# Spreading the inverse softmax sums of two attentions: one rounded, split operand for both heads instead of two fp32 matmuls

## What is computed

```python
def attend(q, k, v, bias=None, mask=None, sink=None):
    s = jnp.einsum('...qngd,...knd->...ngqk', q, k).astype(jnp.float32) * (HEAD_DIM ** -0.5)
    if bias is not None:
        s = s + bias.astype(jnp.float32)
    if mask is not None:
        s = jnp.where(mask, s, NEG_INF)
    if sink is not None:
        s = jnp.concatenate([s, sink_col], axis=-1)
    p = jax.nn.softmax(s, axis=-1)
    ...
    return jnp.einsum('...ngqk,...knd->...qngd', p.astype(v.dtype), v)
```

## Time and profile before

| what | us |
|---|---|
| median of three runs (lowest, highest) | 3851.95 (3849.77, 3854.59) |
| the profiled execution, its own time | 3849.42 |
| its span | 3847.3 |
| TensorE busy in the span | 3714.5 (97%) |
| VectorE busy | 2176.0 (57%) |
| ScalarE busy | 1860.0 (48%) |
| GpSimd busy | 1753.7 (46%) |

### The profile page before, as it was taken

One profiled execution on the slowest core, in us unless ns is written; L12 is line 12 of the kernel. 1 busy time (PEld: TensorE's weight loads), 2 busy tenths in 40 slices (PEclk: granted clock), 3 DMA queues, 4 the chain that ended last, 5 costly groups with the idle time before them and its releaser, 6 DMA issues.

```text
span 3847.3 us, 58742 instructions
## 1 busy us (share of the span) xinstructions
PE 3714.5 (97%) x19908; PEld 3019.3 (78%) x19908; DVE 2176.0 (57%) x3299; ACT 1860.0 (48%) x3560; POOL 1753.7 (46%) x1373
## 2 busy tenths in 40 slices
PE   9998899999999998999999999999999999999999
PEld 7866788788887767887888877788878987678887
DVE  4567642788535676328884864742246856643234
ACT  4555544444445654444444535744445653654343
POOL 4423573556543245645555232065554135025563
PEclk9999999999999989999999999999999999999999
DMA  3210241455222202314542322132223432012222
GB/s 141 93 61 28 72 142 61 159 192 179 93 89 83 71 17 88 137 62 172 191 164 104 137 83 88 40 115 93 98 88 126 175 137 77 6 40 88 98 93 88
DMA packets 107772, 391.64 MB, mean 102 GB/s; under 512 B 11952, under 2 KB 12080, under 8 KB 107184
## 3 DMA queue, kind: packets, MB, share of 16 engines
q1 hardware_dynamic: 88704, 321.95, 23.8%
q10 hardware_dynamic: 16416, 57.62, 4.2%
q0 software_dynamic: 2448, 9.36, 0.6%
HBM read 386.79 MB, written 2.10 MB: 101 GB/s over the span
## 4 chain that ended last, share of the span: by engine, by line
PE 72%; issue 14%; DVE 6%; POOL 5%; ACT 2%; DMA 0%; ACTq 0%; DVEq 0%; POOLq 0%; SPq 0%
PE ps L673 19%; PE ps L675 19%; PE ps L674 19%; POOL arena_parts L637 2%; PE ps L1156 2%; PE ps L1175 1%; POOL arena_parts L641 1%; PE ps L1164 1%; POOL lines L428 1%; PE ps L2175 1%; PE ps L2185 1%; DVE rstd L2110 1%; PE ps L845 1%; PE ps L1134 1%; PE ps L2081 1%
## 5 line engine op out<-in xcount | busy, mean ns | idle before, releaser
L674 PE MATMUL ps<-arena_parts 128*128 128x512 f32 (+1 forms) x3184 | 1184.6, 372 | 0.0
L637 POOL TENSOR_TENSOR arena_parts<-ring,arena_parts 128x512 fp32r<-128x512 f32 x498 | 662.4, 1330 | 1127.3 <-ACT arena_parts L614 920.0
L673 PE MATMUL ps<-h_parts,arena_parts 128*128 128x512 f32 x2128 | 841.9, 396 | 10.0 <-POOL arena_parts L637 7.2
L675 PE MATMUL ps<-h_parts,arena_parts 128*128 128x512 f32 x2128 | 829.4, 390 | 0.0
L641 POOL TENSOR_TENSOR arena_parts<-ring,arena_parts 128x512 fp32r<-128x512 f32 x498 | 672.6, 1351 | 293.0 <-ACT arena_parts L623 292.3
L674 PEld LDWEIGHTS ps<-arena_parts 128*128 128x128 f32 x3184 | 601.0, 189 | 105.5 <-issue 2.6
L614 ACT ACTIVATE arena_parts<-ring 128x512 fp32r<-128x512 f32 x580 | 364.9, 629 | 657.2 <-PE ps L675 598.7
L1653 DVE SCALAR_TENSOR_TENSOR conv<-ps,cols,conv 128x511 f32<-128x511 f32 (+3 forms) x536 | 377.7, 705 | 535.8 <-ACT conv L1668 371.4
L623 ACT ACTIVATE arena_parts<-ring 128x512 fp32r<-128x512 f32 x580 | 363.9, 628 | 604.1 <-PE ps L675 563.4
L673 PEld LDWEIGHTS ps<-h_parts,arena_parts 128*128 128x128 f32 x2128 | 400.2, 188 | 101.6 <-issue 9.7
L675 PEld LDWEIGHTS ps<-h_parts,arena_parts 128*128 128x128 f32 x2128 | 400.2, 188 | 83.7
(11 more groups left out here) (344 smaller groups left out, 6484.5 us busy)
## 6 DMA issues: line engine op xcount, KB each, us to landing
ring<-in_stream SPq DMA_DIRECT2D x612, 512.0 KB, 3.2
ctx<-in_mod ACTq DMA_DIRECT2D x48, 512.0 KB, 3.2
sq<-in_mod ACTq DMA_DIRECT2D x48, 512.0 KB, 3.2
sq<-in_bias POOLq DMA_DIRECT2D x8, 512.0 KB, 4.4
conv<-in_bias POOLq DMA_DIRECT2D x8, 512.0 KB, 4.5
arena<-in_mem ACTq DMA_DIRECT2D x2, 1024.0 KB, 4.8
out_y<-x ACTq DMA_DIRECT2D x8, 256.0 KB, 2.7
x<-in_x SPq DMA_DIRECT2D x4, 256.0 KB, 4.7
```

What stands on the lines that cost most here:

```text
L637: eng.tensor_tensor(side_of(lin, i, c, 0, to), side_of(lin, i, c, 0, raw), side_of(lin, i, c, 0, top), ALU.subtract)\
L673: pe.matmul(out, w_h, x_h, start=start, stop=False)
L674: pe.matmul(out, w_h, x_r, start=False, stop=False)
L675: return pe.matmul(out, w_r, x_h, start=False, stop=stop)
```

## The change

Per block, ScalarE now writes a rounded copy of both heads' inverses, each broadcast to 64 columns, as one 128 x 128 operand (`inverse_high_act`), and VectorE writes the rounded rest (`inverse_rest_dve`). Both are double-buffered in `last512`. TensorE multiplies high and rest with a rounded identity (`eye_r`) over the whole array, accumulating in the same PSUM tile. ScalarE's copy of block n - 1 stands behind its copy of the turned probabilities of n - 1; VectorE's rest of n - 2 stands at the head of its pass n, ahead of `top(n)`. The spread waits for the rest (`inv_rest`) instead of the inverse (`ri_ready`). The rounded identity is a further constant, rounded once by VectorE in the first layer.

```diff
-CONST_NAMES = ["ident", "ones", "blocks", "causal", "anti", "lower", "rot"]
+CONST_NAMES = ["ident", "ones", "blocks", "causal", "anti", "lower", "rot", "eye"]
...
-                pe.wait_ge(S["ri_ready"], D.inv0 + v + 1)
+                pe.wait_ge(S["inv_rest"], D.inv0 - INV_NA + v + 1)
                 wait(pe, D.evac, v)
-                for a in range(2):
-                    mm = pe.matmul(psf[heads_of(a), INVERSE:INVERSE + P], inv2[:, v % 2, a:a + 1].to_broadcast([P, HD]), ident,
-                                   start=True, stop=True)
+                for part, half in enumerate((inv_high, inv_rest)):
+                    mm = pe.matmul(psf[:, INVERSE:INVERSE + P], half(v), eye_r, start=part == 0, stop=part == 1)
                 mm.then_inc(S["inv_spread"], 1)
...
+        inv_high, inv_rest = (lambda v, i=i: last512[:, (2 * i + v % 2) * P:(2 * i + v % 2 + 1) * P] for i in range(2))
...
+        def inverse_high_act(act, D, n):
+
+            v = D.block_done(n)
+            if v is None:
+                return
+            act.wait_ge(S["ri_ready"], D.inv0 + v + 1)
+            wait(act, "inv_spread", D.inv0 - INV_NA + v - 1)
+            act.activation(by_head(inv_high(v)), inv2[:, v % 2, :].unsqueeze(2).to_broadcast([P, 2, HD]), ACT.Copy).then_inc(S["inv_high"], 1)
+
+        def inverse_rest_dve(dve, D, n):
+
+            v = D.block_done(n)
+            if v is None:
+                return
+            dve.wait_ge(S["inv_high"], D.inv0 - INV_NA + v + 1)
+            dve.tensor_tensor(by_head(inv_rest(v)), inv2[:, v % 2, :].unsqueeze(2).to_broadcast([P, 2, HD]), by_head(inv_high(v)).bitcast(F32),
+                               ALU.subtract).then_inc(S["inv_rest"], 1)
...
             def inverse(v):
                 dve.wait_ge(S["p_done"], U_NA + v + 1)
+                wait(dve, "inv_rest", NA.inv0 - INV_NA + v - 1)
                 dve.reciprocal(inv2[:, v % 2, :], sum2[:, v % 2, :]).then_inc(S["ri_ready"], 1)
...
             for n in range(N + 3):
+                if 2 <= n < N + 2:
+                    inverse_rest_dve(dve, NA, n - 2)
                 if n < N:
                     top(n)
...
                 if n > 0:
                     duo_copy_act(act, NA, n - 1)
+                    inverse_high_act(act, NA, n - 1)
...
                     dve.wait_ge(S["tables_in"], 16)
+                    dve.tensor_copy(eye_r, K("eye")).then_inc(S["eye_ready"], 1)
                     rope_dve(dve)
```

More of the change, by code:

```diff
@@ L204, in build @@
         arena_parts, sq_parts, rstd_parts = rounded("arena", [P, ARENA]), rounded("sq", [P, 4, SEQ]), rounded("rstd", [P, SEQ])
+        const_parts = rounded("const", [P, N_CONST])
         ps = stack.enter_context(nc.psum_tensor("ps", [P, 8, 512], F32))
@@ L225, in build @@
         ident, ones = K("ident"), K("ones")
+        eye_r = const_parts[:, CONST_AT["eye"]:CONST_AT["eye"] + P]
         xbc = cut(0, XBC, SEQ)
@@ L305, in build @@
                      "cs_ready", "y_done", "y_evac", "yz_ready", "cond_ready", "mod_step", "mod_turned", "mod_folded", "mod_summed",
-                     "mod_ready", "gain_ready", "qsq_ready", "qsq_mm", "qstd_ready", "qrstd_ready", "rot_mm",
-                     "rot_cos", "rot_sin", "roped", "shifted", "inv_spread", "inv_row", "sink_exp", "sum_ready", "mo_evac", "na_evac", "swa_evac", "o_high", "o_rest", "mo_high",
+                     "mod_ready", "gain_ready", "qsq_ready", "qsq_mm", "eye_ready", "qstd_ready", "qrstd_ready", "rot_mm",
+                     "rot_cos", "rot_sin", "roped", "shifted", "inv_high", "inv_rest", "inv_spread", "inv_row", "sink_exp", "sum_ready", "mo_evac", "na_evac", "swa_evac", "o_high", "o_rest", "mo_high",
                      "k_proj", "lat_high", "lat_rest", "mw_high", "mw_rest", "pre_high", "pre_rest", "pre_rows", "pre_scaled", "nsink_ready"):
@@ L2209, in duo_pe @@
             N = len(D.units)
+            pe.wait_ge(S["eye_ready"], 1)
             for name, value in D.ready:
@@ L2239, in duo_copy_act, with by_head @@
             act.activation(D.cut(D.probT, n), D.turned(n), ACT.Copy).then_inc(S["pt_ready"], 1)
+        inv_high, inv_rest = (lambda v, i=i: last512[:, (2 * i + v % 2) * P:(2 * i + v % 2 + 1) * P] for i in range(2))
+        def by_head(t):
+            return t.rearrange("p (a d) -> p a d", a=2)
+        def inverse_high_act(act, D, n):
[12 more added lines that the diff above has]
+                               ALU.subtract).then_inc(S["inv_rest"], 1)
         def duo_out_dve(dve, D, v):
@@ L2433, in inverse @@
                 dve.wait_ge(S["sum_ready"], v + 1)
+                wait(dve, "inv_rest", SWA.inv0 - INV_NA + v - 1)
                 dve.reciprocal(inv2[:, v % 2, :], sum2[:, v % 2, :]).then_inc(S["ri_ready"], 1)
@@ L2444, in swa_dve @@
             for n in range(N + 3):
+                if 2 <= n < N + 2:
+                    inverse_rest_dve(dve, SWA, n - 2)
                 if n < N:
@@ L2469, in swa_act @@
                     duo_copy_act(act, SWA, n - 1)
+                    inverse_high_act(act, SWA, n - 1)
                 if n % per == 3 and n > per:
@@ L3123, in pack_constants @@
     half = HD // 2
+    put("eye", i == j)
     put("rot", np.where((i // HD == j // HD) & (j % HD < half) & (i % HD == j % HD + half), -1.0, 0.0)
```

## The result

| | before | changed |
|---|---|---|
| median, us | 3852.1 | 3959.29 |
| lowest to highest | 3849.77 to 3854.59 | 3953.69 to 3962.85 |
| span of the profiled execution | 3847.3 | 3957.2 |

The ratio is 1.0277, with a 95% interval of 1.0264 to 1.029: 107 us slower, where 98 were forecast.

The account below looks back on a forecast made before the run. TensorE was taken to bound both attentions. Serial waits added 65.6 and 34.2 us, together 99.8, or 98 after first-turn and last-block corrections, with TensorE's gain worth nothing: 3852 + 98 = 3950 us, range 3925 to 3990.

Parts of the forecast that it names:

- The forecast's signs: If right, attentions take about 203 and 182 us, TensorE busy near two thirds; if wrong, clock near 0.5 for long.
- The ring: Both attentions: exponentials, copy, H, R, next maximum, next exponentials run in series; +98 us, chance 0.76.
- H: ScalarE's added rounded 128 x 128 copy of the inverses, per block: 0.31 us.
- R: VectorE's added 128 x 128 subtraction for the rounded rest, per block: 0.25 us until the next instruction.
- The first attention: Neighbourhood attention: a pair of heads goes from 17.36 to 25.56 us, +65.6 us over 8 pairs.
- The second attention: Sliding-window attention: a pair of heads goes from 17.88 to 22.16 us, +34.2 us over 8 pairs.
- The fallen clock: Rival: idle TensorE drops to half clock in a third of 96 units, +35 to +58 us more, about 3995; chance 0.11.
- The likeliest case: The series of waits in both attentions as sized, with no clock loss: 3950 us, chance 0.76.
- TensorE's gain: Rounded pair for the spread: -8 to +5 us over 80 blocks, -4 taken, only if TensorE stays last.
- the gap: TensorE's 0.17 us issue gap ahead of the spread should move behind it; counted at nothing.
- TensorE stays last: Rival: VectorE's new wait is empty and only the matmul pair counts, about 3844 us; chance 0.04.
- A half-open ring: Rival: only wide-to-wide steps couple fully, or hand-overs overlap more; +20 to +70 us, about 3900; chance 0.07.

Follow-up runs that it names:

- opening it: The changed kernel with VectorE's subtraction for unit n - 2 behind the maximum of unit n instead of ahead of it, in both attentions: 3860.95 us.
- taking one member out: The changed kernel with ScalarE's rounded copy of the inverses ahead of its copy of the turned probabilities instead of behind it: 3886.49 us.
- doubling one: The changed kernel with ScalarE's rounded copy of the inverses done twice, order otherwise unchanged: 3972.27 us.
- the filler: The changed kernel with one further fp32 128 x 512 matmul ahead of the transposes of wide units, except short-step units of the sliding-window attention: 3944.9 us.
- open in both places: The changed kernel with the subtraction behind the maximum and ScalarE's rounded copy ahead of its copy of the turned probabilities: 3850.84 us.
- the old matmuls: The changed kernel, order unchanged, with TensorE's two fp32 matmuls of before in place of the rounded pair: 3945.54 us.

## Why the prediction was right, and where it was off

**The sum** was nearer than its parts: the first attention came out 6 us under its forecast and the second 14 over, so that the total is only 9 us off is partly luck. The forecast's signs name 203 and 182 us for the stages; these are counted from the shorter windows of the earlier trace rows (137 and 148), so its 203 and the 206.1 measured over the whole stage are not the same length, and the growths are what can be compared.

**The ring** was the step that carried it, and it held: opening it gives back 98 us, taking one member out shortens a wide step by that member's 0.92 us, and doubling one lengthens it by 0.20. H measured 0.31 us and R 0.29, the next instruction starting 0.21 later: the forecast had 0.31 and 0.25.

**The first attention** was to grow by 65.6 less about 1 us and grew by 58.8. The step between wide units is 4.79 us and not 4.97, and the other steps of a pair are about as much shorter: 24.46 us for a pair at full clock, not 25.56. The 0.18 is the overlap of queued instructions on ScalarE and VectorE: the copy starts 1.34 us after the first exponential (2371.10 to 2372.44), not 1.45 plus a hand-over, because it now finds its input ready; and R counts 0.21, not 0.25. In the earlier trace rows the copy had waited for TensorE, so that row could not show the overlap.

**The second attention** was to grow by about 33 us and grew by 47.4. With the clock held by the filler it grows by 34.2 (190.6 us), so the ring was sized about right there too, and the 13.2 us above it are the clock's. One term of that sum was wrong all the same. The step from the second 640 block's first head to its second head was put at 3.74 us and takes 4.82, at full clock. ScalarE's copy waits there for TensorE's transposes:

```profile
3448.22 0.41 PE L2198 MATMUL ps<-const_parts,arena_parts 128*128 128x128 f32 x2 [0.59 <-DVE h L2272]
```

```profile
3449.56 0.79 ACT L2233 ACTIVATE arena<-ps,top 128x640 f32<-128x640 f32 x1 [0.33 <-DVE top L2453]
...
3451.66 0.70 ACT L2241 ACTIVATE arena<-ps 128x640 f32<-128x640 f32 x1 [1.03 <-PE ps L2187]
...
3454.38 0.79 ACT L2233 ACTIVATE arena<-ps,top 128x640 f32<-128x640 f32 x1 [1.30 <-DVE top L2453]
```

TensorE is late because its spread waits for the output of the block before (`D.evac`), and that output stands behind the late maximum on VectorE. From the spread at 3448.22 on it works without a pause up to those transposes. In the kernel before, the spread waited for this output twice in both attentions, for 1.1 us together. Now it does so 47 times for 53.7 us, 11 times for 12.4 us of them in the second attention. The forecast had "its 3.2 us per wide unit fit into 4.97" for the first attention, and never set TensorE's work against the short steps of a 640 block. This step alone costs 1.1 us more per pair. The other five steps are each 0.07 to 0.22 shorter than forecast and take half of it back: a pair at full clock takes 22.68 us where 22.16 were forecast.

**The fallen clock** had a chance of 0.11 and +35 to +58 us, for a third of the 96 units. It came, in a smaller size: by the filler's kernel 13 us in the second attention and none that shows in the first. In the second attention four pairs behind the first take up to 4.5 us longer than 22.68. The likeliest case and this rival were not exclusive, and should have been summed as one with a size. Two of the forecast's signs missed mostly for this reason: TensorE is busy for 77% and 82% and not near two thirds, since at half clock the same work keeps it busy longer, and the clock near 0.5, named as a sign of being wrong, stood there for 6 to 17 us at a time while the ring held.

**TensorE's gain** was put at 4 us with bounds of -8 and +5, worth nothing behind the ring. Per block it is 0.05 us on the chain, 4 us over 80, where TensorE is last; by the pairs of heads it is some 3. Loads of the two 128-column operands start 0.11 us apart (two loads in 0.30 us, each 0.19). That agrees with the 107 ns that the prediction worked out from the Trainium skill for such a load (TensorE: Matmul & The Clock Gate, LDWEIGHTS). The prediction's estimate from it, two loads of 107 ns and so no gain, was too strict: the chain has 0.17 us for the pair and not 0.21. That the gap would move and not vanish was right; the two 0.15 us above show it. The Trainium skill's rule that a change of tiling mode drains TensorE (TensorEngine Tiling (Array Packing), Key Properties) agrees with that; that a drain is what fills the gap, no run here shows.

**The other rivals.** "TensorE stays last" with 3844 us needs the ring open; with it open in both places the kernel reaches 3850.84, not told from before. "A half-open ring", 3900, is nearly what the kernel with one member out of the ring takes, 3886.

## What to carry to other kernels

When an instruction is added to an in-order engine, write down what it waits for and what stands behind it, and follow that round until you are back; two engines that ran side by side may now run in turn, and the price is the sum of their work, not the 0.3 us that was added. Placing the waiting instruction behind the work that others wait for, and the producer ahead of the long work that nobody waits for, took back all 107 us. (It took back no more: the kernel with both moves can't be told from the kernel before, and the 3 us that the rounded pair is worth stay below what the whole time shows.) Check the forecast for the steps of each unit and not for their mean, and ask what TensorE's clock will do with the idle time that a ring leaves it.

## What was unexpected of the hardware

The granted clock fell without a long pause. Before the fall at about 3420 us TensorE's longest idle time since 3408 was 1.44 us, and it had been busy for some three quarters of the time; the pause that went ahead of the fall at 3278 us in the kernel before was 2.39 us long. Stretches of 2 us of the changed kernel (us, PE busy, granted clock):

```profile
3416.00:3418.00 2.00, 1.72 (x13) 1.00 0.00 0
3418.00:3420.00 2.00, 0.82 (x8) 0.92 0.00 0
3420.00:3422.00 2.00, 2.00 (x15) 0.50 0.00 0
3422.00:3424.00 2.00, 2.00 (x6) 0.50 0.00 0
3424.00:3426.00 2.00, 2.00 (x14) 0.50 0.03 8
3426.00:3428.00 2.00, 2.00 (x16) 0.87 0.00 0
```

It then stayed at 1.2 GHz for some 6 us although TensorE was busy throughout. And with the rounded pair, which has fewer passes, it fell more often in the same ring than with the old matmuls: in the second attention in four pairs behind the first against none (clock 0.87 against 0.94). These are one profiled execution each, but all four times with the old matmuls (3942.71 to 3948.97 us) lie below all with the pair. Work saved on an engine that is no longer last can cost time through its clock.
